# Convolution input turned and copied by halves of its output, with three reorderings around the down products

## The chip, the cores and the metric

The kernel runs on one core of a Trainium2 chip. The metric is the device time of one execution in microseconds (us). Engines are named as the profile names them: PE is TensorE (PEld its weight loads), DVE is VectorE, ACT is ScalarE, POOL is GpSimd, SP is SyncE, which issues the weight transfers here.

## The reference, cut to what matters

The program is a first transformer block followed by a block of two layers, over 256 tokens and 1024 channels, all in float32. The change touches one layer of the second block (it runs twice) and the last product of the first block:

```python
for i in range(2):                                     # second block
    h = h + 0.5 * swiglu(rms_norm(h), w_gate_up, w_down)      # "a", hidden width 2816
    u = rms_norm(h)
    q, k, v, ca, cg = split(u @ w_in)
    attn = sliding_window_attention(q, k, v)           # 8 heads of 64: 512 channels
    conv = silu(layer_norm(depthwise_conv31(ca * sigmoid(cg))))   # 512 channels, causal, 31 taps
    mixed = concat(rms_norm(attn), rms_norm(conv))
    h = h + mixed @ w_out
    h = h + 0.5 * swiglu(rms_norm(h), w_gate_up, w_down)      # "b"
    h = h + sigmoid(h @ w_gate) * rms_norm(p @ w_ple)
```

The first block ends with `h = h + square(relu(hn @ w_ff1)) @ w_ff2`, hidden width 4096.

## The kernel before, in words

**Weight products.** Every product with a weight matrix is a "chunk" (L2063 to L2087): 256 rows by 512 columns accumulated in one of two PSUM tiles `acc`, over k-tiles of 128. A float32 product is made of three matmuls (high by high, high by low, low by high: L2084 to L2086) for each of two row tiles, so 6 matmuls for a k-tile. Weights come in units of two k-tiles (12 matmuls). For each unit SP loads it into one of 8 `stage` slots (L550), ACT rounds it to `w_hi` (L671), DVE subtracts to `w_lo` (L1265), in one of 4 slots that PE must have used. All queues take the units in one fixed order. `Lout_a0` and `Lout_a1` (attention half of `w_out`), `Lout_c0` and `Lout_c1` (convolution half) and `Lple0`, `Lple1` have two units each, `Lb_up0` four.

**Turns.** Where a product needs its left side transposed, PE transposes 128 by 128 pieces into one of two PSUM banks `turn` (`turned`, L2089 to L2098), four pieces or 512 columns to a bank; ACT copies the bank out rounded (L741, L744), DVE writes the remainder (L1317, L1321). `turn_free` tells PE that a bank was read. The waits `ready(kt)` put such work between the k-tiles of a chunk.

**The convolution** (`conv`, L2510; `conv_round`, L2501). Two taps are applied by one matmul: `u_t` holds the turned input in quads of 32 partitions, 2k and 2k+1 being the same 32 channels shifted by one token. A round is 8 products on 64 rows by 32 columns of the array, side by side. The 8 channel groups fall in two halves of the output (`half`); each half takes 14 rounds with the diagonal weights `diag` and one with `y_late`, in which DVE has applied the last taps (`late_pair`, L1929 to L1938). The float32 round is recorded as 16 matmuls, the whole convolution as 480 in each layer. Before it, PE turns `u` in two banks (L2560), runs `Lple1`, waits until both are copied to `u_t`, and turns the attention output (`Lmixed`, L2564). Bank k holds channel tiles 2k and 2k+1, that is the quads 2k and 2k+1 of both halves, so that a half needs both banks. ACT makes half of the copies of each bank (L1178), DVE the other half (L1924), 4 copies of 32 by 512 each; DVE waits for ACT's and frees the bank (L1927 to L1929).

**After the convolution** ACT and DVE write `y` (L1193, L1951); PE runs `Lout_a0` with the mean over the channels between its k-tiles, then `Lout_a1`. ACT takes silu of `y` tile by tile and rounds it to `x_hi` (L1208, L1212), DVE writes `x_lo` (L1972), PE runs `Lout_c0` with the row means (L2598) between its units, then `Lout_c1`. ACT and DVE split both units of `Lout_c0` (L1204, L1968) before these loops, and DVE adds the result of `Lout_a0` to `h` (L1339) between its split and its loop.

**Boundaries** (`rms_boundary`, L703 on ACT, L1287 on DVE): at the end of a chunk pair DVE adds the second product to `h`, PE turns `h`, and the splits of the next chunk lie around this. `early` is 1 only where the last chunk has fewer than 4 units, which is `Lout_c1`.

**The last hidden turn.** A down product (`d0` in the first block, `La_dn0` and `Lb_dn0` in each layer) starts with hidden tiles that are already turned; the last hidden chunk is turned from inside it, when kt is UNIT_K = 2 (L2428 `last_ff`, L2475 `last_hid`), after waiting for DVE's L1765 or L1816.

## Time and profile before

| | us |
|---|---|
| median of 3 runs | 1474.58 (1474.26 to 1478.44) |
| profiled execution | 1474.51 |
| its span, first to last instruction | 1472.7 |
| PE busy | 1436.9 (98% of the span) |
| DVE busy, ACT busy | 878.1 (60%), 802.2 (54%) |
| DMA | 170 GB/s mean, queue q1 at 53.5% |
| granted TensorE clock, mean | 0.993 |

The second block's layers occupy about 450 to 960 and 960 to 1465 us of the span; the attention and convolution of the first lie at 648 to 735 us, those of the second at 1159 to 1246 us. Times below are us from the start of the span. A mean clock of 0.993 says that the engine ran at its upper level, 2.4 GHz, nearly all the time; 0.50 in a window is the lower level, 1.2 GHz. In a timeline row the first number is the start, the second the length of the group, the one in brackets the engine's idle time before it and what ended that.

### The profile page before, as it was taken

The numbers are of one execution on the slowest core, as the hardware profiler recorded it, in microseconds if no ns is written. First come the engines' busy times: TensorE is split into PE (matmuls) and PEld (weight loads), VectorE is DVE, ScalarE is ACT, GpSimd is POOL, SyncE is SP. The second block draws the span as 40 slices with busy tenths as digits, with TensorE's granted clock in tenths as the row PEclk, the third lists the DMA queues.
The fourth block names the chain that finished last, engine by engine and source line by source line (L and its number), as shares of the span: only waits on it lengthen the run. The fifth ranks groups of instructions, "written<-read, shape, count | busy, mean of one in ns | idle before, by whom it ended". The sixth has DMA issues, their size and how long they took to land.

```text
span 1472.7 us, 20845 instructions
## 1 busy us (share of the span) xinstructions
PE 1436.9 (98%) x7848; PEld 1185.6 (81%) x7848; DVE 878.1 (60%) x1154; ACT 802.2 (54%) x1227; POOL 15.8 (1%) x29
## 2 busy tenths in 40 slices
PE   8899999999999999999999999999999999999997
PEld 7788888888888888887788888888888877888885
DVE  4776766665545556556565555655564665655555
ACT  6678764654346444466564544564444765544444
POOL 2000000000000000000000000000000000000000
PEclk9999999999999999999999999999999999999998
DMA  9663354655666665552266656566555433665550
GB/s 244 198 210 115 115 176 153 214 175 168 194 189 206 185 182 179 161 169 96 88 209 185 185 176 205 177 187 185 185 185 158 144 115 100 199 185 183 189 188 29
DMA packets 133163, 249.89 MB, mean 170 GB/s; under 512 B 8752, under 2 KB 16496, under 8 KB 133088
## 3 DMA queue, kind: packets, MB, share of 16 engines
q1 hardware_dynamic: 131520, 245.09, 53.5%
q0 software_dynamic: 1360, 3.70, 1.3%
q8 instruction: 51, 0.84, 0.2%
q14 instruction: 24, 0.20, 0.0%
q10 hardware_dynamic: 208, 0.06, 0.0%
HBM read 247.77 MB, written 1.05 MB: 169 GB/s over the span
## 4 chain that ended last, share of the span: by engine, by line
PE 93%; DVE 2%; DMA 1%; ACT 1%; SPq 1%; issue 1%; DVEq 0%; ACTq 0%
PE acc L2084 28%; PE acc L2086 27%; PE acc L2085 27%; PE turn L2097 5%; PE pair L2506 2%; PE turn L2146 1%; DMA stage<-in_w_in 1%; PE pair L2125 1%; DVE w_lo L1265 1%; PE pair L2572 0%; SPq L550 0%; PE pair L2119 0%; DVE u_t L1924 0%; SPq L554 0%; ACT w_hi L671 0%
## 5 line engine op out<-in xcount | busy, mean ns | idle before, releaser
L1265 DVE TENSOR_TENSOR w_lo<-stage,w_hi 128x1024 fp32r<-128x1024 f32 (+2 forms) x480 | 563.9, 1184 | 396.5 <-ACT w_hi L671 391.5
L671 ACT ACTIVATE w_hi<-stage 128x1024 fp32r<-128x1024 f32 (+2 forms) x480 | 487.4, 1028 | 469.0 <-PE acc L2086 461.5
L2084 PE MATMUL acc<-w_hi,x_hi 128*128 128x512 f32 (+2 forms) x1296 | 514.0, 397 | 7.6 <-DVE w_lo L1265 5.0
L2086 PE MATMUL acc<-w_hi,x_lo 128*128 128x512 f32 (+2 forms) x1296 | 501.7, 387 | 0.0
L2085 PE MATMUL acc<-w_lo,x_hi 128*128 128x512 f32 (+2 forms) x1296 | 501.1, 387 | 0.0
L2084 PEld LDWEIGHTS acc<-w_hi,x_hi 128*128 128x128 f32 x1296 | 244.3, 188 | 58.2 <-issue 7.1
L2086 PEld LDWEIGHTS acc<-w_hi,x_lo 128*128 128x128 f32 x1296 | 244.0, 188 | 51.0
L2085 PEld LDWEIGHTS acc<-w_lo,x_hi 128*128 128x128 f32 x1296 | 244.6, 189 | 45.8 <-issue 0.2
L2084 PE MATMUL acc<-w_hi,g_hi 128*128 128x512 f32 x352 | 137.7, 391 | 0.0
L2086 PE MATMUL acc<-w_hi,g_lo 128*128 128x512 f32 x352 | 137.1, 389 | 0.0
L2085 PE MATMUL acc<-w_lo,g_hi 128*128 128x512 f32 x352 | 137.0, 389 | 0.0
L2086 PEld LDWEIGHTS acc<-w_hi,g_lo 128*128 128x128 f32 x352 | 66.1, 188 | 13.8
L2084 PEld LDWEIGHTS acc<-w_hi,g_hi 128*128 128x128 f32 x352 | 66.1, 188 | 13.6
L2085 PEld LDWEIGHTS acc<-w_lo,g_hi 128*128 128x128 f32 x352 | 66.1, 188 | 13.4
L744 ACT ACTIVATE x_hi<-turn,vec 128x256 fp32r<-128x256 f32 x72 | 28.6, 474 | 46.0 <-PE turn L2097 45.9
L2084 PE MATMUL acc<-w_hi,f_hi 128*128 128x512 f32 x128 | 50.0, 390 | 0.0
L2086 PE MATMUL acc<-w_hi,f_lo 128*128 128x512 f32 x128 | 49.8, 389 | 0.0
L2085 PE MATMUL acc<-w_lo,f_hi 128*128 128x512 f32 x128 | 49.8, 389 | 0.0
L1321 DVE SCALAR_TENSOR_TENSOR x_lo<-turn,vec,x_hi 128x256 fp32r<-128x256 f32 x72 | 30.0, 477 | 25.4 <-ACT x_hi L744 25.4
L1317 DVE TENSOR_TENSOR g_lo<-turn,g_hi 128x512 f32 (+1 forms) x44 | 30.0, 682 | 18.6 <-ACT g_hi L741 18.6
L1816 DVE SCALAR_TENSOR_TENSOR hid<-acc,stat,silu 128x256 f32<-128x256 f32 x88 | 38.2, 476 | 2.8 <-ACT silu L700 2.8
L741 ACT ACTIVATE g_hi<-turn 128x512 f32 (+1 forms) x44 | 26.3, 598 | 24.5 <-PE turn L2097 24.5
(323 smaller groups left out, 1146.9 us busy)
## 6 DMA issues: line engine op xcount, KB each, us to landing
stage<-in_ffn_w_gate_up SPq DMA_DIRECT2D x176, 512.0 KB, 3.7
stage<-in_ffn_w_down SPq DMA_DIRECT2D x88, 512.0 KB, 4.0
stage<-in_w_in SPq DMA_DIRECT2D x64, 512.0 KB, 4.3
stage<-in_w_ff SPq DMA_DIRECT2D x64, 512.0 KB, 4.3
stage<-in_w_out SPq DMA_DIRECT2D x16, 512.0 KB, 3.8
stage<-in_w_ple_gate SPq DMA_DIRECT2D x16, 512.0 KB, 4.5
stage<-in_w_lru_up SPq DMA_DIRECT2D x8, 512.0 KB, 4.1
stage<-in_w_o SPq DMA_DIRECT2D x8, 512.0 KB, 4.4
```

The costliest lines, as they stand in the source:

```text
L671: act.activation(w_hi[:, n.slot(SPLIT), 0:t, 0:w], stage[:, n.slot(STAGE), 0:t, 0:w], ACT.Copy).then_inc(hi_done, 1)
L741: act.activation(dst[:, bass.ds(at, 2), :], bank, ACT.Copy).then_inc(turn_hi, 1)
L744: ins = act.activation(dst[:, at + i, :], bank[:, i, :], ACT.Copy, scale=gain[:, at + i:at + i + 1])
L1265: dve.tensor_tensor(w_lo[:, n.slot(SPLIT), 0:t, 0:w], stage[:, n.slot(STAGE), 0:t, 0:w], w_hi[:, n.slot(SPLIT), 0:t, 0:w].bitcast(F32), AL ...
L1317: dve.tensor_tensor(lo[:, bass.ds(at, 2), :], bank, hi[:, bass.ds(at, 2), :].bitcast(F32), ALU.subtract).then_inc(turn_free[n.slot(2)], 1)
L1321: ins = dve.scalar_tensor_tensor(lo[:, at + i, :], bank[:, i, :], gain[:, at + i:at + i + 1], hi[:, at + i, :].bitcast(F32), ALU.mult, ALU ...
L1816: ins = dve.scalar_tensor_tensor(hid2[:, i % 2, t, :], acc[b][:, t, HALFW:COLS], stat[:, t:t + 1], silu[:, i % 2, t, :], ALU.mult, ALU.mult)
L2084: pe.matmul(dst, xh, wh, start=kt == 0, stop=False)
L2085: pe.matmul(dst, xh, wl, start=False, stop=False)
L2086: mm = pe.matmul(dst, xl, wh, start=False, stop=kt == last)
L2097: mm = pe.transpose(turn[n.slot(2)][0:cols_in, at:at + rows_in], src, ident[0:rows_in, 0:rows_in])
L2506: mm = pe.matmul(pair[c * QUAD:(c + 1) * QUAD, k, half * S:(half + 1) * S], weights(rows_in, n), src(rows_in, n), start=first, stop=last)
```

## The change

1. `u` is turned by halves: bank 0 gets channel tiles 0 and 2, bank 1 tiles 1 and 3, so that the bank holds all that one half of the convolution needs. A copy to `u_t` is 32 by 256 instead of 32 by 512, and ACT and DVE make 8 for a bank instead of 4 (`shifted_pairs`).
2. PE no longer waits for both banks ahead of the convolution. Each half waits for its own bank. The turns of `Lmixed`, which need both banks free, move from ahead of the convolution to between the 14 rounds of half 0 and its last round.
3. `Lout_c0`: ACT splits unit 1 after the third silu and second `x_hi` instead of ahead of the loop; DVE splits unit 1 after the second `x_lo`.
4. DVE's `rms_boundary` with `early` = 1 (`Lb_norm` only) adds the residual of `Lout_c1` before it splits unit 1 of `Lb_up0`, no longer after it.
5. The last hidden turn of `d0` and of each `dn0` moves from kt = 2 to kt = 4.

```diff
@@ -528,11 +528,14 @@
             for k in range(max(0, count - 2), count):
                 turn_read(eng, name, k, layer)
 
-        def shifted_pair(k, c, i):
-
-            quad = 2 * k + i
-            dst = u_t[quad * QUAD:(quad + 1) * QUAD, c::KC, TAPS2 - 1 - i:TAPS2 - 1 - i + S]
-            return dst, lambda bank: bank[c * QUAD:(c + 1) * QUAD, :].rearrange("p (n s) -> p n s", n=2)
+        def shifted_pairs(half, blocks, bank):
+
+            for c in blocks:
+                for k in range(2):
+                    for i in range(2):
+                        quad, at = 2 * k + i, TAPS2 - 1 - i
+                        yield (u_t[quad * QUAD:(quad + 1) * QUAD, half * KC + c, at:at + S],
+                               bank[c * QUAD:(c + 1) * QUAD, k * S:(k + 1) * S])
 
         block = ctx.enter_context(nc.Block())
 
@@ -1172,10 +1175,8 @@
                 for k in range(2):
                     n = TURNS.at("Lu", k, layer)
                     wait(act, turn_done, n + 1)
-                    for c in range(KC // 2):
-                        for i in range(2):
-                            copy_to, copy_from = shifted_pair(k, c, i)
-                            ins = act.activation(copy_to, copy_from(turn[n.slot(2)]), ACT.Copy)
+                    for copy_to, copy_from in shifted_pairs(k, range(KC // 2), turn[n.slot(2)]):
+                        ins = act.activation(copy_to, copy_from, ACT.Copy)
                     ins.then_inc(s_shifted, 1)
                 for k in range(2):
                     turned_hi(x_hi, "Lmixed", k, vec2[:, layer, V2["attn"]:V2["attn"] + 4], layer)
@@ -1201,7 +1202,7 @@
                 act.wait_ge(s_sqattn, layer + 1)
                 rows = stat[:, STATS["attn"]:STATS["attn"] + TT]
                 act.activation(rows, rows, ACT.Sqrt, bias=eps).then_inc(s_rattn, 1)
-                split("Lout_c0", layer)
+                split("Lout_c0", layer, units=[0])
                 wait(act, s_yn, Count(1, [(layer, 1)]))
                 for n in range(KC + 1):
                     if n < KC:
@@ -1211,6 +1212,8 @@
                         wait(act, s_silu, Count(n, [(layer, KC)]))
                         act.activation(x_hi[:, 4 + n - 1, :], y[:, n - 1, :], ACT.Copy,
                                        scale=vec2[:, layer, V2["conv"] + n - 1:V2["conv"] + n]).then_inc(s_convhi, 1)
+                    if n == 2:
+                        split("Lout_c0", layer, units=[1])
                 act.activation(ysq[:, :, :], y[:, :, :], ACT.Square).then_inc(s_ysq, 1)
                 embedding_squares(1)
                 wait(act, score_done, SCORES.at("Lsum", 3, layer))
@@ -1299,9 +1302,9 @@
                 for k in (0, 1):
                     turned_lo(hi, lo, norm, k, gain, layer)
                 split(parts[1], layer, units=range(min(n_last, a + 3), n_last))
-                split(first, layer, units=range(early, 2))
+                split(first, layer, units=range(early, 2 - early))
                 add_residual(parts[1], 1, scale, layer)
-                split(first, layer, units=range(2, 3))
+                split(first, layer, units=range(2 - early, 3))
                 for k in (2, 3):
                     turned_lo(hi, lo, norm, k, gain, layer)
                 split(first, layer, units=range(3, U))
@@ -1918,10 +1921,8 @@
                 for k in range(2):
                     n = TURNS.at("Lu", k, layer)
                     wait(dve, turn_done, n + 1)
-                    for c in range(KC // 2, KC):
-                        for i in range(2):
-                            copy_to, copy_from = shifted_pair(k, c, i)
-                            ins = dve.tensor_copy(copy_to, copy_from(turn[n.slot(2)]))
+                    for copy_to, copy_from in shifted_pairs(k, range(KC // 2, KC), turn[n.slot(2)]):
+                        ins = dve.tensor_copy(copy_to, copy_from)
                     link(ins)
                     wait(dve, s_shifted, Count(k + 1, [(layer, 2)]))
                     dve.sem_inc(turn_free[n.slot(2)], 1)
@@ -1965,12 +1966,14 @@
                 wait(dve, s_rattn, Count(1, [(layer, 1)]))
                 at = STATS["attn"]
                 link(dve.reciprocal(stat[:, at:at + TT], stat[:, at:at + TT]))
-                split("Lout_c0", layer)
+                split("Lout_c0", layer, units=[0])
                 add_residual("Lout_a0", 0, stat[:, at:at + TT], layer)
                 for n in range(KC):
                     wait(dve, s_convhi, Count(n + 1, [(layer, KC)]))
                     dve.scalar_tensor_tensor(x_lo[:, 4 + n, :], y[:, n, :], vec2[:, layer, V2["conv"] + n:V2["conv"] + n + 1],
                                              x_hi[:, 4 + n, :].bitcast(F32), ALU.mult, ALU.subtract).then_inc(s_convlo, 1)
+                    if n == 1:
+                        split("Lout_c0", layer, units=[1])
                 add_residual("Lout_a1", 1, stat[:, at:at + TT], layer)
 
                 def conv_factors():
@@ -2425,7 +2428,7 @@
                 if kt == 0:
                     for m in range(2):
                         turn_read(pe, "ff", 2 * (NF - 2) + m)
-                elif kt == UNIT_K:
+                elif kt == 2 * UNIT_K:
                     ff_turns(NF - 1)
                 elif kt == KF1 - COLS // P:
                     for m in range(2):
@@ -2476,7 +2479,7 @@
 
                     if kt == 0:
                         turn_read(pe, f"L{f}_hid", UPS - 2, layer)
-                    elif kt == UNIT_K:
+                    elif kt == 2 * UNIT_K:
                         hid_turns(UPS - 1)
                     elif kt == KF2 - HALFW // P:
                         turn_read(pe, f"L{f}_hid", UPS - 1, layer)
@@ -2510,9 +2513,13 @@
                 def conv():
 
                     for half in range(2):
+                        turn_read(pe, "Lu", half, layer)
                         for j in range(PAIRS_PE):
                             conv_round(half, lambda rows_in, n: diag[rows_in, n, j, :],
                                        lambda rows_in, n: u_t[rows_in, n, 2 * j:2 * j + S], j == 0, False)
+                        if half == 0:
+                            turns_read(pe, "Lu", 2, layer)
+                            turn_rows("Lmixed", mixo2, 2, layer)
                         wait(pe, s_late_taps, Count(half + 1, [(layer, 2)]))
                         mm = conv_round(half, lambda rows_in, n: quad_ident[rows_in, :],
                                         lambda rows_in, n: y_late[rows_in, n, :], False, True)
@@ -2557,11 +2564,10 @@
                 turn_read(pe, "Lp", 0, layer)
                 chunk("Lple0", pl_hi, pl_lo, layer)
                 evacuated(pe, "Lca", layer)
-                turn_rows("Lu", u, 2, layer)
+                for half in range(2):
+                    turned("Lu", half, [u[:, t, f * P:(f + 1) * P] for f in (half, 2 + half) for t in range(TT)], layer)
                 chunk("Lple1", pl_hi, pl_lo, layer)
-                turns_read(pe, "Lu", 2, layer)
                 wait(pe, s_mixo, Count(2, [(layer, 1)]))
-                turn_rows("Lmixed", mixo2, 2, layer)
                 wait(pe, s_diag, Count(1, [(layer, 1)]))
                 free(SCORES, score_free, "Lsum", 0, layer)
                 conv()
```

## Rows read from the trace of the kernel before

**Rows 1.** The page: busy time of each engine, its share, and instructions.
```profile
PE 1436.9 (98%) x7848; PEld 1185.6 (81%) x7848; DVE 878.1 (60%) x1154; ACT 802.2 (54%) x1227; POOL 15.8 (1%) x29
```

**Rows 2.** Waits of PE, 230 to 1460 us: in total, times, longest.
```profile
PE turn L2097 <- DVEq L1927: 5.9, 2, 3.0
PE turn L2097 <- issue: 4.7, 7, 1.1
```

**Rows 3.** Timeline around the convolution, first layer.
```profile
687.55 2.80 DVE L1924 COPY u_t<-turn 32x512 f32<-32x512 f32 x4 [2.91 <-PE turn L2097]
688.07 4.79 ACT L1178 ACTIVATE u_t<-turn 32x512 f32<-32x512 f32 x8
...
693.58 1.94 PE L2097 MATMUL turn<-ct,mixo 128*128 128x128 f32 x8 [2.96 <-DVEq L1927]
...
695.45 7.00 PE L2506 MATMUL pair<-u_t,diag 64*32 64x256 f32 x224
...
710.86 0.19 PEld L2084 LDWEIGHTS acc<-w_hi,x_hi 128*128 128x128 f32 x1 [0.41 <-issue]
```

**Rows 4.** Windows: length, PE busy and instructions, then clock, DMA share, GB/s last.
```profile
693.50:695.50 2.00, 1.92 (x16) 1.62 (x20) 1.90 (x6) 0.80 (x2) 0.00 (x0) 0.52 0.03 8
695.50:711.00 15.50, 14.79 (x482) 10.17 (x482) 8.70 (x18) 7.04 (x15) 0.00 (x0) 0.95 0.34 105
...
1205.60:1221.80 16.20, 15.89 (x483) 10.27 (x483) 9.93 (x22) 7.74 (x18) 0.00 (x0) 0.90 0.32 100
...
354.00:356.00 2.00, 0.86 (x8) 1.00 0.95 331
```

**Rows 5.** Tile `y`: durations (min/median/max ns) of reads of 128x256 from PSUM.
```profile
L1193 ACT ACTIVATE y<-pair,vec x4: 467/472/475, 711.0 to 1221.8; 128x256 f32<-128x256 f32 x4
L1951 DVE TENSOR_SCALAR y<-pair,vec x4: 473/480/485, 711.0 to 1221.8; 128x256 f32<-128x256 f32 x4
```

**Rows 6.** Timeline of ACT and DVE beside the convolution, first layer.
```profile
693.57 1.14 DVE L1935 TENSOR_SCALAR pt<-u_t,taps 128x256 f32<-128x256 f32 x4 [0.18 <-DVE u_t L1924]
...
694.70 1.69 ACT L744 ACTIVATE x_hi<-turn,vec 128x256 fp32r<-128x256 f32 x4 [1.84 <-PE turn L2097]
...
696.34 2.35 DVE L1265 TENSOR_TENSOR w_lo<-stage,w_hi 128x1024 fp32r<-128x1024 f32 x2
...
702.35 0.21 ACT L1127 ACTIVATION_READ_ACCUMULATOR hid<-e_ple 128x1 f32 x1
```

**Rows 7.** Timeline around `Lout_c0`, first layer.
```profile
722.40 2.36 DVE L1265 TENSOR_TENSOR w_lo<-stage,w_hi 128x1024 fp32r<-128x1024 f32 x2
...
722.64 1.09 ACT L1208 ACTIVATE y<-y,vec 128x256 f32<-128x256 f32 x2
...
726.22 1.04 ACT L1214 ACTIVATE sm<-y 128x1024 f32<-128x1024 f32 x1
...
726.86 0.47 PE L2084 MATMUL acc<-w_hi,x_hi 128*128 128x512 f32 x1 [1.29 <-DVE x_lo L1972]
...
728.50 1.28 ACT L1217 ACT_TABLE_LOAD   x1
...
732.79 2.36 DVE L1265 TENSOR_TENSOR w_lo<-stage,w_hi 128x1024 fp32r<-128x1024 f32 x2 [3.56 <-ACT w_hi L671]
```

**Rows 8.** Timeline at the end of `Lout_c1`, first layer.
```profile
741.40 1.23 DVE L1265 TENSOR_TENSOR w_lo<-stage,w_hi 128x1024 fp32r<-128x1024 f32 x1 [1.24 <-ACT w_hi L671]
...
742.54 1.40 DVE L1339 SCALAR_TENSOR_TENSOR h<-acc,stat,h 128x512 f32<-128x512 f32 x2
...
744.11 1.06 PE L2097 MATMUL turn<-ct,h 128*128 128x128 f32 x8 [0.61 <-issue]
```

**Rows 9.** Timeline at the start of `d0`.
```profile
351.37 0.39 PE L2084 MATMUL acc<-w_hi,f_hi 128*128 128x512 f32 x1
...
355.39 1.06 PE L2097 MATMUL turn<-ct,hid 128*128 128x128 f32 x8 [1.14 <-issue]
...
358.12 1.22 DVE L1265 TENSOR_TENSOR w_lo<-stage,w_hi 128x1024 fp32r<-128x1024 f32 x1
```

## The prediction

> **What bounds the kernel now.** The page first: PE is busy 98% of the span, DVE and ACT 60% and 54% [rows 1]. PE sets the time, so the change can only gain by what PE stands still or runs slowly, and all of it is worth reading one by one. The waits of PE between 230 and 1460 us come next [rows 2]. Two kinds matter: 5.9 us in two waits behind L1927, where DVE frees the banks of `u`, and 4.7 us in seven waits ahead of a turn that the profile calls "issue". The timelines tell what those seven are: one of 1.14 at `d0` [rows 9], two of 0.61 at the `Lb_norm` boundary [rows 8], and the other four are the last hidden turns of the `dn0` chunks: (4.7 - 1.14 - 1.22) / 4 = 0.58 each. In all of them PE waits for a DVE result that comes just too late. A last one stands ahead of `Lout_c0`, 1.29 us, for `x_lo` [rows 7]. Then the windows for the clock [rows 4]: it falls to its lower level only around the convolution, after PE stood still for 2.96 us [rows 3].
>
> The profiled execution (1474.51, span 1472.7) is within 0.1 us of the median of the runs, so the sum is made against 1474.5. What a measurement of this kernel can tell from no change is about 0.3%, 4.4 us.
>
> **1. The wait ahead of the convolution.** Before: `Lple1` ends at 693.58 - 2.96 = 690.62, the turns of `Lmixed` begin at 693.58, the convolution runs from 695.45 to 710.86, 15.4 us [rows 3]. After, PE needs only bank 0. ACT starts to copy at 688.07 and DVE at 687.55, as now. They make 8 copies of 32x256 each. No row has that copy. Bounds: not under half of today's 32x512, 4.79/8 = 0.60 on ACT and 2.80/4 = 0.70 on DVE [rows 3], which is 0.30 and 0.35; not above the whole, 0.60 and 0.70. The nearest rows are the reads of 128x256 from PSUM, also in pairs, 472 ns on ACT and 480 on DVE alone [rows 5], and two of them back to back take 0.84 and 0.88, so 0.42 and 0.44 a piece. I take these: ACT ends at 688.07 + 8 x 0.42 = 691.4, DVE at 691.1, and PE goes 0.2 later as now (693.39 to 693.58), at 691.6. The stall is 1.0 instead of 2.96: 2.0 gained.
> The two banks together now cost 16 x 0.44 = 7.0 on DVE and not 5.8, and 6.7 on ACT and not 4.8. The copy of half a row at 0.42 instead of 0.30 shows a fixed cost for each instruction. The Trainium skill (VectorE: DVE Perf Modes, the section on the TRN2 errata) has the same rule against small pieces and gives 120 and 172 fixed cycles for a read from PSUM. From its figures the pieces would be 0.39 on DVE and 0.36 on ACT, an estimate that would let PE start 0.5 us earlier and make the result 1461.3; it also puts today's 32x512 at 0.66 and 0.57, under the 0.70 and 0.60 of the trace, so I stay with the rows.
>
> **2. The clock.** In the first layer the granted clock is 0.52 over 2.0 us and 0.95 over 15.5: 1.9 + 1.55 = 3.5 us at 1.2 GHz. In the second it is 0.90 over 16.2 us: 3.2 us [rows 4]. Work done at half speed costs half of that, 1.7 us a layer. It begins right behind the 2.96 us of idle time. Idle times of 1.14 (in the window from 354, at 1.00 [rows 4]) and 1.29 us bring no fall, and the new stall is 1.0, so I count it as gone: 1.65 a layer.
>
> **3. The turns of `Lmixed` in the convolution.** Their 1.06 us at full clock stay PE work. What is new is that PE leaves the 64x32 tiles and comes back. The only row of such a switch is the first full weight load behind the convolution, 0.41 idle [rows 3]; I put two switches at 0.4 together, bounds 0 and 0.8.
> Nothing else may wait. DVE finishes bank 1 at 691.2 + 3.5 = 694.9 with its handovers; the late taps of a half take 693.57 to 696.34 = 2.8 [rows 6], so those of half 0 are there at 697.9. PE comes to them at 691.6 + 14 rounds + turns. The convolution at full clock is 15.4 less 0.8 (half of 1.55) = 14.6 with 0.9 of gaps in the first layer, 13.7 without: 30 rounds of 0.46. So half 0 ends at 698.0, the turns at 699.2: DVE is early by 1.3, and that is what moving the turns there covers. The half-1 taps follow after the split of `Lout_a0`, at 697.9 + 2.35 + 2.8 = 703.1; PE wants them at 705.9.
> On ACT everything behind `turned_hi` for `Lmixed` is queued behind the later turns: 694.70 to 702.56, 7.9 us [rows 6]. It now begins at 698.8 and ends at 706.7; PE ends the convolution at about 707. ACT then writes `y`. It is a tie, with 0.4 us more before PE asks for `y` (one k-tile of `Lout_a0`, 6 matmuls, comes first). I count nothing.
> Together, a layer: 2.0 + 1.65 - 0.4 - 0.2 for ties and handovers = 3.0. Check by positions: PE at 690.6 + 1.0 + 13.7 + 0.9 + 1.1 + 0.4 = 707.7 against 710.9, 3.2. I take 3.0; two layers, **6.0**. Bounds, for the two layers: 1.2 (copies as dear as today's, a stall of 2.7, half of the clock's gain, 0.4 for the switches) and 9 (copies at half of today's, a stall of 0.1, free switches).
>
> **4. `Lout_c0`.** DVE now does one unit (1.18, half of 2.36) from 722.40, the residual of 1.4, and the first `x_lo` of 0.48: it ends at 725.6 and not 726.7, and PE starts 1.1 earlier. The second split goes between; PE needs it two k-tiles later, at 728.5. ACT: the first silu no longer waits for a second split (it starts at 722.3, when `y` is ready, not 722.64), but the loop to 726.22 grows by 1.0 for the split, so the squares L1214 run from 726.9 to 728.0, just ahead of the row means at 728.5; the unit's `w_hi` is done at 725.8 and `w_lo` at 727.3. Next late is ACT's table load: now at 728.50, then at 729.3 to 730.6, which puts the square root and the first split of `Lout_c1` at 730.8. Its `w_lo`, now at 732.79, starts at 731.9. So 0.9 of the 1.1 is kept [rows 7]. Two layers, **1.8**, bounds 0.5 and 2.6.
>
> **5. The boundary.** A unit is four half k-tiles of 3 matmuls: in `d0` two k-tiles take 354.25 - 351.37 = 2.88 with the tail of the last matmul, 2.75 from start to start [rows 9]. PE ends the first unit of `Lb_up0` at 744.11 - 0.61 = 743.5 [rows 8], so `Lout_c1` ended at 740.65. DVE today waits for `w_hi` (741.3), splits to 742.54, adds to 743.94, and PE turns at 744.11. After: the residual runs at 740.85 to 742.25, the split at 742.3 to 743.5, and PE needs both. It waits for the split, to 743.65. Gain 0.45; two layers, **0.9**, bounds 0 and 1.2.
>
> **6. The hidden turns.** At kt = 4 the DVE result is over 2 us old, so the whole idle time goes: 1.14 + 4 x 0.58 = **3.5**. Cover for it is the unit of weight work now put ahead of the turn. Behind it are ACT's and DVE's copies of the turn and then the fifth unit's split, queued behind the later turn: in `d0` its `w_lo` starts at 358.12 now [rows 9], then about 359.7 and is done at 360.9. PE asks for it at kt = 8, 351.4 + 8 k-tiles of 1.375 + 1.06 = 363.4 [rows 9]. Free by 2.5 us. The turned tile itself is used near the end of the chunk.
>
> No weight load moves in the order of SP. The loads follow DVE's splits, and at 53% of the DMA there is room for a kernel under 1% shorter.
>
> **Sum.** 6.0 + 1.8 + 0.9 + 3.5 = 12.2. 1474.5 - 12.2 = **1462.3**.
>
> **The rivals.**
> - *The clock still falls.* The short stall is followed by work on small tiles. For: in the second layer it fell about 1 us after PE had restarted. Against: idle times of 1.1 and 1.3 us without a fall. Price 1.65 x 2: 1465.6. Chance 0.12. The Trainium skill (TensorE: Matmul & The Clock Gate, the section on what is happening) says that the point of change shifts with where the work lands; this trace has it at two different points.
> - *Copies do not get cheaper by halves.* 0.60 and 0.70: bank 0 is done at 693.2, the stall is 2.7 and the clock falls again. (1.7 + 1.65) x 2 lost: 1469.0. Chance 0.04.
> - *Something is late next.* ACT's tie in part 3, its squares or table load in part 4, or a fifth unit in part 6; each would take 1 to 3.5 back, say 1464.8. Chance 0.12.
> - *Slower: the clock stays low through the convolution.* With turns in the middle and 64x32 tiles at both sides PE might be granted 1.2 GHz for all of `conv`: at half speed its 13.7 us of work take 27.4, so 1462.3 + 2 x 13.7 = 1489.7. It ends above the time of before once the loss is over 12.2 / 2 = 6.1 us a layer, that is once the low clock lasts over 12.2 us in each. Against: the convolution now runs at 1.00 for its last 12 us, on the same tiles. Chance 0.02.
>
> **How the numbers follow.** My forecast has 0.70. The range goes down by what cheaper copies and free switches could add, and part of the spread of part 4, to 1459.5, and up over the clock and the late rivals to 1467.0; copies at today's price and the slow case stay outside. Faster by over 0.3% (under 1470.1) holds all but the slow rival and some of the unseen: 0.94, same 0.03, slower 0.03.
>
> **What would show it.** Right: waits behind DVE at the start of `conv` of about 1.0 and not 2.96; windows there at 1.00; no idle time ahead of the `hid` turns; idle ahead of `Lout_c0` under 0.3 and about 0.3 ahead of `Lout_c1`; 32x256 copies of 0.42 to 0.44. Wrong: a clock of 0.5 in the convolution, a wait of L2506 for the late taps, ACT's `y` starting over 0.4 us after the last round, or a stall at kt = 8 of a `dn0`.

## The result, and the profile after

The changed kernel takes 1458.76 us (median of 4 runs, 1457.99 to 1459.28) against 1474.76 before (median of 4): ratio 0.989, 95% interval 0.9872 to 0.9907, so 16.0 us faster. Beside other kernels later it took 1458.33 against 1473.53, ratio 0.9896 (0.9875 to 0.9917). The forecast was 1462.3 with a range from 1459.5 to 1467.0: the direction and the places were right, the gain of 12.2 was a quarter too small, and the result lies 0.7 us under the range. The changed kernel's profiled execution took 1459.28, its span is 1457.5.

The page of the changed kernel, busy time ([rows 1] before), then its waits of PE between 225 and 1450 us, in total, times, longest ([rows 2]):

```profile
PE 1432.0 (98%) x7848; PEld 1185.7 (81%) x7848; DVE 880.2 (60%) x1170; ACT 803.6 (55%) x1243; POOL 15.8 (1%) x29
```

```profile
PE pair L2509 <- DVEq L1928: 1.4, 2, 0.7
PE pair L2509 <- issue: 0.6, 1, 0.6
PE acc L2087 <- DVE x_lo L1973: 0.3, 2, 0.2
PE turn L2100 <- DVE w_lo L1268: 0.3, 2, 0.2
```

Five of the seven waits ahead of turns are gone and the two at the boundary have shrunk from 0.61 to 0.16; the wait for the banks has shrunk from 5.9 to 1.4, that for `x_lo` from 2.6 to 0.3. One line names no other engine: 0.6 "issue" inside the convolution, idle time of PE for which the profile shows no cause; below it is called a gap. The kernel before has such gaps too:

```profile
PE pair L2506 <- issue: 0.9, 2, 0.6
```

The timeline around the convolution, first layer, changed kernel ([rows 3] and [rows 6]); PE, DVE and ACT:

```profile
686.35 3.49 DVE L1925 COPY u_t<-turn 32x256 f32<-32x256 f32 x8 [2.90 <-PE turn L2100]
686.87 6.15 ACT L1179 ACTIVATE u_t<-turn 32x256 f32<-32x256 f32 x16
690.05 3.49 DVE L1925 COPY u_t<-turn 32x256 f32<-32x256 f32 x8 [0.21 <-ACT u_t L1179]
...
690.11 6.28 PE L2509 MATMUL pair<-u_t,diag 64*32 64x256 f32 x224 [0.70 <-DVEq L1928]
693.73 1.14 DVE L1936 TENSOR_SCALAR pt<-u_t,taps 128x256 f32<-128x256 f32 x4 [0.18 <-DVE u_t L1925]
...
696.32 1.09 PE L2100 MATMUL turn<-ct,mixo 128*128 128x128 f32 x8
...
697.02 1.57 ACT L747 ACTIVATE x_hi<-turn,vec 128x256 fp32r<-128x256 f32 x4 [4.00 <-PE turn L2100]
697.35 0.18 PEld L2509 LDWEIGHTS pair<-pt,vec 64*32 64x32 f32 x16 [0.17 <-issue]
...
703.35 1.73 PE L2509 MATMUL pair<-u_t,diag 64*32 64x256 f32 x54 [0.63 <-issue]
...
705.66 0.50 PE L2087 MATMUL acc<-w_hi,x_hi 128*128 128x512 f32 x1
705.80 0.84 ACT L1194 ACTIVATE y<-pair,vec 128x256 f32<-128x256 f32 x2 [1.06 <-PE pair L2509]
```

The copies of one bank take 3.49 on DVE (0.44 a piece) and half of 6.15 on ACT (0.38 a piece). PE begins the convolution 0.70 after `Lple1`, turns `Lmixed` in the middle with nothing idle on either side, and ACT is free 1.06 before it may write `y` (in the second layer 0).

Windows of the changed kernel over the convolution and its turns, both layers ([rows 4]): length, then busy time and instructions of PE, PEld, DVE, ACT, POOL, then granted clock, DMA share, GB/s:

```profile
690.10:705.60 15.50, 14.86 (x488) 11.21 (x488) 13.96 (x31) 10.56 (x24) 0.00 (x0) 1.00 0.23 73
1194.00:1208.20 14.20, 14.20 (x488) 10.95 (x488) 13.82 (x31) 10.12 (x23) 0.00 (x0) 1.00 0.24 77
```

The clock is at its upper level in both windows. (In both kernels it also stands at 1.2 GHz at about 50 us, 0.55 and 0.53 granted between 49 and 56 us, and at the very end; no part of the change is there.) The same 488 instructions take 1.3 us longer in the first layer; an experiment below bears on why.

The other places in the changed kernel: `Lout_c0` and its splits ([rows 7]), the boundary ([rows 8]) and the turn in `d0` ([rows 9]):

```profile
717.12 1.10 ACT L1209 ACTIVATE y<-y,vec 128x256 f32<-128x256 f32 x2 [0.65 <-DVE y L1964]
...
719.41 1.05 ACT L674 ACTIVATE w_hi<-stage 128x1024 fp32r<-128x1024 f32 x1
...
720.52 0.47 PE L2087 MATMUL acc<-w_hi,x_hi 128*128 128x512 f32 x1 [0.16 <-DVE x_lo L1973]
720.69 1.22 DVE L1268 TENSOR_TENSOR w_lo<-stage,w_hi 128x1024 fp32r<-128x1024 f32 x1
...
725.23 0.26 ACT L1220 ACTIVATE stat<-pair,ct 128x2 f32<-128x2 f32 x1
...
726.48 2.36 DVE L1268 TENSOR_TENSOR w_lo<-stage,w_hi 128x1024 fp32r<-128x1024 f32 x2 [2.46 <-ACT w_hi L674]
...
737.32 1.09 PE L2100 MATMUL turn<-ct,h 128*128 128x128 f32 x8 [0.16 <-DVE w_lo L1268]
...
357.74 1.03 PE L2100 MATMUL turn<-ct,hid 128*128 128x128 f32 x8
...
359.35 2.01 ACT L674 ACTIVATE w_hi<-stage 128x1024 fp32r<-128x1024 f32 x2
```

**Where the time went.** Both kernels run the same 5616 weight matmuls in the same order, so the difference in the start times of the same matmul can be followed through the program. It is flat, to 0.05 us, between the edited places, and steps at them. (The first 90 us differ from one execution to the next; there the changed kernel's execution lost 0.93.)

| place | forecast | step, layer 1 | step, layer 2 | sum |
|---|---|---|---|---|
| convolution, last matmul of `Lple1` to first of `Lout_a0` | 3.0 a layer | 4.00 | 4.68 | 8.7 |
| `Lout_c0` | 0.9 a layer | 1.12 | 1.10 | 2.2 |
| boundary `Lb_norm` | 0.45 a layer | 0.42 | 0.43 | 0.85 |
| hidden turn of `d0` | 1.14 | 1.34 | | 1.3 |
| hidden turns of the `dn0` | 0.58 each | 0.73, 0.74 | 0.74, 0.73 | 2.9 |

The sum is 16.0. What is left open is why each is larger than its row of idle time.

### The profile page after: what moved, and what is told of

It reads as the page before. It is cut to its first block, busy times and chain, and to the rows that moved or that the text cites. A ratio compares the mean times of both kernels' runs of the same rounds, so it can differ in the third digit from the quotient of the medians.

```text
span 1457.5 us, 20877 instructions
## 1 busy us (share of the span) xinstructions
PE 1432.0 (98%) x7848; PEld 1185.7 (81%) x7848; DVE 880.2 (60%) x1170; ACT 803.6 (55%) x1243; POOL 15.8 (1%) x29
## 4 chain that ended last, share of the span: by engine, by line
PE 93%; DVE 2%; ACT 2%; DMA 1%; SPq 1%; issue 1%; DVEq 0%; ACTq 0%
PE acc L2087 28%; PE acc L2089 27%; PE acc L2088 27%; PE turn L2100 5%; PE pair L2509 2%; PE turn L2149 1%; DMA stage<-in_w_in 1%; PE pair L2128 1%; DVE w_lo L1268 1%; ACT w_hi L674 1%; PE pair L2578 0%; SPq L553 0%; ACT u_t L1179 0%; PE pair L2122 0%; SPq L557 0%
```

## The experiments

The theory to begin with: (a) the standstill itself makes the clock fall, and both together are most of the gain; (b) a wait that vanishes is worth more than its idle time; (c) nothing is taken back by leaving the small tiles. Its rivals stand in the expectations. "Stage" below is the time from the last matmul of `Lple1` to the first of `Lout_a0`, start to start; "work" is the part of it from the first turn of `Lmixed` or the first round; "start to start" is the time between the starts of two matmuls.

| kernel | wait, layers 1 and 2 | work, layer 1 | work, layer 2 |
|---|---|---|---|
| before | 2.96, 2.96 | 17.29 | 16.71 |
| changed | 0.70, 0.70 | 15.55 | 14.30 |
| both banks awaited | 4.48, 4.47 | 15.67 | 15.99 |
| order of before, new copies | 4.48, 4.48 | 18.32 | 17.50 |
| before, wait filled | 1.64 after the filling | 14.45 | 15.42 |
| one more switch | 0.70, 0.70 | 15.23 | 14.62 |
| loads held back | 0.70, 0.70 | 14.31 | 14.30 |
| input turned earlier, first and second run | none | 14.59, 14.38 | 14.35, 14.30 |

### Both banks awaited

```diff
                 free(SCORES, score_free, "Lsum", 0, layer)
+                turns_read(pe, "Lu", 2, layer)
                 conv()
```

> The changed kernel, but PE waits for both banks of the turned input ahead of the convolution; the turns of Lmixed stay in its middle. Both theories: the convolution starts when DVE has copied the second bank, 693.54 + 0.27 = 693.8 instead of 690.1, so 3.7 us more a layer. Theory (the clock falls because PE stands still for some us): it falls again at the start of the convolution, for some 3.3 us at 1.2 GHz in each layer, 1.65 more a layer, together 10.7 over the changed kernel: 1469.5. Rival (the fall came from the turns that stood between the wait and the convolution, and these are gone from there): the clock stays at 1.00 and the time is 1458.8 + 7.4 = 1466.2.

Measured: 1468.81 (10 runs), ratio to before 0.9966 (0.9952 to 0.998). Windows over the convolution of this kernel:

```profile
691.60:707.20 15.60, 15.59 (x488) 10.92 (x488) 10.55 (x23) 7.32 (x15) 0.00 (x0) 0.91 0.26 77
1199.40:1215.40 16.00, 15.95 (x488) 12.12 (x488) 10.58 (x23) 7.36 (x15) 0.00 (x0) 0.89 0.25 73
```

PE waits 4.5 us and the clock falls again, without any turn between wait and convolution: in both layers 3.41 us at 1.2 GHz (added up from windows of 0.5 us). The rival falls. The stage is 5.5 longer in the second layer, near what was expected (3.8 of waiting and 1.7 of clock), and 3.9 in the first, where the gap of the changed kernel is missing and part of the low clock lay in the wait.

### Order of before, new copies

```diff
-                        if half == 0:
-                            turns_read(pe, "Lu", 2, layer)
-                            turn_rows("Lmixed", mixo2, 2, layer)
...
+                turns_read(pe, "Lu", 2, layer)
+                turn_rows("Lmixed", mixo2, 2, layer)
                 conv()
```

> The changed kernel with PE's order of before around the convolution (both banks, then the turns of Lmixed, then all rounds), so only the smaller copies are left of that part. Theory (a 32x256 copy carries most of the cost of a 32x512 one): both banks take 16 x 0.436 on DVE, 7.0 and not 5.8, PE stands still for 4.3 us a layer instead of 2.96, and the stage is 1.4 us a layer slower than in the kernel before; the rest of the change keeps its gain of about 7.4: near 1470.2. Rival (halves cost no more in sum, since the engines are bound by the elements): the stage is as before, 1467.4.

Measured: 1471.94 (10 runs), ratio 0.9983 (0.9968 to 0.9997). Its waits, and a window of the second layer:

```profile
PE turn L2100 <- DVEq L1928: 9.0, 2, 4.5
PE pair L2509 <- issue: 1.7, 2, 1.4
```

```profile
1204.10:1221.60 17.50, 17.29 (x488) 11.14 (x488) 10.51 (x23) 7.83 (x16) 0.00 (x0) 0.84 0.30 93
```

The wait is 1.52 longer than before, so halving the copies alone is a loss, and the longer wait costs clock too: in the second layer 6.8 us at 1.2 GHz. The stage is 2.6 and 2.3 us slower a layer than in the kernel before, not 1.4: the theory is right, its size was off by the gaps (1.4 and 0.3 idle in the first layer here) and, in the second layer, by the clock. Only together with the reordering do the smaller copies pay.

### The wait filled in the kernel before

```diff
                 chunk("Lple1", pl_hi, pl_lo, layer)
+                free(SCORES, score_free, "Lsum", 0, layer)
+                keep_warm(12)
                 turns_read(pe, "Lu", 2, layer)
                 wait(pe, s_mixo, Count(2, [(layer, 1)]))
                 turn_rows("Lmixed", mixo2, 2, layer)
                 wait(pe, s_diag, Count(1, [(layer, 1)]))
-                free(SCORES, score_free, "Lsum", 0, layer)
```

> The kernel before, with 12 transposes of the identity into an unused part of PSUM in the wait of PE ahead of the turns of Lmixed, so that PE is busy in it; nothing else is changed. Theory (the standstill makes the clock fall): PE starts the turns at the same place, the clock stays at 1.00 in the convolution, and the 3.5 and 3.2 us at 1.2 GHz cost nothing: 1.7 a layer less, 1474.7 - 3.4 = 1471.3. Rival (the fall comes with the small tiles or by chance): the clock falls as before and the time is 1474.7, or more if the transposes last longer than the wait.

Measured: 1470.76 (10 runs), ratio 0.9982 (0.9966 to 0.9997). The windows of this kernel over the wait of the first layer and over both convolutions, then PE's timeline in the wait:

```profile
691.00:694.10 3.10, 1.51 (x13) 1.23 (x11) 2.77 (x4) 2.37 (x5) 0.00 (x0) 1.00 0.00 0
694.10:708.60 14.50, 14.45 (x489) 11.44 (x489) 10.60 (x23) 7.72 (x16) 0.00 (x0) 1.00 0.37 113
1202.20:1217.60 15.40, 14.88 (x488) 10.45 (x488) 10.61 (x23) 7.72 (x16) 0.00 (x0) 1.00 0.34 105
```

```profile
691.03 1.47 PE L2154 MATMUL pair<-ct 128*128 128x128 f32 x12
694.15 1.06 PE L2097 MATMUL turn<-ct,mixo 128*128 128x128 f32 x8 [1.64 <-issue]
695.14 6.27 PE L2506 MATMUL pair<-u_t,diag 64*32 64x256 f32 x224
701.21 0.63 PE L2506 MATMUL pair<-pt,vec 64*32 64x256 f32 x16
701.64 6.38 PE L2506 MATMUL pair<-u_t,diag 64*32 64x256 f32 x221
```

The turns start at the same distance from `Lple1` as before (3.35 us), the wait is as long, but half of it is filled with useless work, and the clock stays at 1.00. The stages are shorter by 2.8 and 1.3 us, together 4.1. This isolates the clock: 3.41 us at half speed cost 1.7 us in each layer of the kernel before, 3.4 in all, and it was the standstill that brought them; the rest, and the uneven shares, are gaps in the issue (one of 0.43 in the second layer here). An idle time of 1.64 us did not.

One trace stands for each kernel here, and the fall need not come in every execution. The medians differ by 2.5 us (1473.21 against 1470.76), less than the 4.1 of the two traces. The 43 executions of the kernel before that were timed beside these kernels spread from 1468.4 to 1478.9 us: 11 with a mean granted clock of 0.995 or more took 1468.4 to 1473.5, 13 with 0.992 or less 1472.8 to 1478.9. Ten executions of the changed kernel lie between 1456.9 and 1459.3, all at 0.995 or 0.996. The low stretch at the start of the program varies too (3.4 to 6.8 us in a piece), so the mean clock alone does not tell where the clock fell.

This trace also gives the price of the place of the turns. With the turns ahead, from their start to the first round of half 1 it takes 701.64 - 694.15 = 7.49 us, in both layers. With the turns between rounds 14 and 15 it takes 697.80 - 690.11 = 7.69 in the changed kernel, in both layers and in both of its traces:

```profile
697.80 4.92 PE L2509 MATMUL pair<-u_t,diag 64*32 64x256 f32 x164
```

So leaving the small tiles and coming back costs 0.2 us a layer, though the profile shows nothing idle there. The rest of the work takes 6.61 where there is no gap. At the upper clock and without gaps the order of before would thus need 14.1 us (7.49 + 6.61) and the changed one needs 14.30. What is above that and above the 1.7 of the clock is gaps: 1.5 and 0.9 us in the two layers of the kernel before, 1.25 and 0 in the changed one.

### Hidden turns back

```diff
-                elif kt == 2 * UNIT_K:
+                elif kt == UNIT_K:
                     ff_turns(NF - 1)
...
-                    elif kt == 2 * UNIT_K:
+                    elif kt == UNIT_K:
                         hid_turns(UPS - 1)
```

> The changed kernel with the last hidden turn of d0 and of each dn0 back at kt = 2. The forecast's sum takes the idle time of the waits as the price: 1.14 + 4 x 0.58 = 3.5, so 1462.3. Theory (a stall costs more than the idle time shown, since a matmul's recorded 0.39 overlaps the next by 0.16 and the pipeline restarts): 1.41 in d0 and 0.74 in each dn0, 4.4 in all, 1463.2. In the trace the first matmul after the turn would stand 1.4 and 0.75 later against the matmul before it than in the changed kernel.

Measured: 1461.39 (4 runs), ratio 0.9915 (0.9887 to 0.9943). Its timeline in `d0`:

```profile
354.76 1.06 PE L2100 MATMUL turn<-ct,hid 128*128 128x128 f32 x8 [1.14 <-issue]
```

Idle times of 1.14 and 0.58 are back, and the start times step by 1.34 and by 0.74, 0.75, 0.75, 0.77: 4.35 in all. The theory holds on the size. Weight matmuls follow each other at 0.23 us but are recorded as 0.39 long, so the idle time in the profile begins 0.16 late, and each wait that vanishes is worth 0.16 to 0.2 more than it shows.

### Splits of `Lout_c0` back, boundary back

```diff
-                split("Lout_c0", layer, units=[0])
+                split("Lout_c0", layer)
...
-                    if n == 2:
-                        split("Lout_c0", layer, units=[1])
```

(the same on DVE), and in the other kernel

```diff
-                split(first, layer, units=range(early, 2 - early))
+                split(first, layer, units=range(early, 2))
                 add_residual(parts[1], 1, scale, layer)
-                split(first, layer, units=range(2 - early, 3))
+                split(first, layer, units=range(2, 3))
```

> The changed kernel with both units of Lout_c0 split ahead of the loops again, on ACT and on DVE. Theory (a wait costs its idle time and the 0.16 by which a recorded matmul overlaps the next, and ACT's table load takes nothing back): the stage from Lout_a1 to the start of Lout_c1 is 1.12 longer in each layer, 2.2 in all. Rival, as the forecast had it (the table load makes the first split of Lout_c1 late and takes 0.2 back): 0.9 a layer, 1.8 in all.

> The changed kernel with DVE's split of unit 1 of Lb_up0 ahead of the residual again. Forecast and theory agree: 0.42 to 0.45 longer a layer at the turn in Lb_up0, 0.85 in all, with an idle time of 0.6 ahead of that turn. Rival (the gain there came from the earlier stages): nothing is lost.

Measured, one time each: 1462.61 and 1458.33, with the first 90 us of the span 1.4 longer in the one and 1.5 shorter in the other than in the changed kernel's first trace. The steps against the changed kernel are clean: 1.13 and 1.12 at `Lout_c0` in the first, 0.44 and 0.44 at the turn in `Lb_up0` in the second. The waits of the first show what came back:

```profile
PE acc L2083 <- DVE x_lo L1971: 2.6, 2, 1.3
```

Nothing is taken back by the table load: in the changed kernel it ends at 725.22, just as the row means do, the square root follows at 725.23, and the first `w_lo` of `Lout_c1` is done at 727.7, 0.2 before PE starts that chunk at 727.9.

### One more switch of tiles

```diff
                         for j in range(PAIRS_PE):
+                            if half == 0 and j == 10:
+                                turns_read(pe, "Lu", 2, layer)
+                                turned("Lmixed", 0, pieces(mixo2, 0), layer)
                             conv_round(...)
                         if half == 0:
-                            turns_read(pe, "Lu", 2, layer)
-                            turn_rows("Lmixed", mixo2, 2, layer)
+                            turned("Lmixed", 1, pieces(mixo2, 1), layer)
```

> The changed kernel with the two turns of Lmixed at two places of half 0, after 10 rounds and after 14, so that PE leaves the small tiles once more and comes back; the work is the same. Forecast (two switches cost 0.4): 0.4 longer a layer. Theory (a switch costs nothing that can be read, since the convolution of the changed kernel shows no gap at its own): under 0.1 a layer, apart from gaps in the issue of the convolution, which vary from 0 to 1.3 us from run to run.

Measured: 1460.92, one time. Work in the second layer 14.62 against 14.30. PE's timeline there:

```profile
1195.40 4.55 PE L2509 MATMUL pair<-u_t,diag 64*32 64x256 f32 x160 [0.70 <-DVEq L1928]
1199.88 0.66 PE L2100 MATMUL turn<-ct,mixo 128*128 128x128 f32 x4
1200.47 1.96 PE L2509 MATMUL pair<-u_t,diag 64*32 64x256 f32 x64
1202.36 0.66 PE L2100 MATMUL turn<-ct,mixo 128*128 128x128 f32 x4
1202.95 0.66 PE L2509 MATMUL pair<-pt,vec 64*32 64x256 f32 x16
```

In the first layer the work is 15.23, as in three kernels with one switch less (hidden turns, splits and boundary back: 15.23, 15.22, 15.23), but with a gap that is 0.3 shorter. Leaving the tiles and coming back once more costs 0.3 in the layer without gaps, half of it in the turns themselves (0.59 + 0.59 start to start, against 1.02 for both together). The theory's "under 0.1" is wrong as a general price; 0.4 was nearly right for a second switch. At the place of the change the price is the 0.2 us read from the kernel with the filled wait.

### Loads held back

```diff
+                wait(sp, s_conv, Count(1, [(layer, 1)]))
                 swiglu_loads("b", layer)
```

> The changed kernel, but SP holds the loads of Lb_up0 back until the convolution is over. Theory on the gaps in the issue of the convolution (0.9 to 1.3 in the first layer of most traces, with no wait on another engine): the fetch of PE's instructions is late behind the burst of weight loads at 698 to 703 us. Then the convolution with its turns takes 14.3 in the first layer too, 0.9 to 1.2 less, and nothing else changes. Rival (the gaps have nothing to do with the loads): they stay, 15.2 to 15.6 in the first layer.

Measured: 1457.6, one time. In the changed kernel the gap follows a stretch in which the weight queue fills the DMA engines and one fetch of instructions (q8) stands between its packets. The DMA queues there, 700 to 702 us: packets, MB, share:

```profile
q1 hardware_dynamic: 382, 0.75, 99.0%
q8 instruction: 1, 0.02, 2.7%
```

With the loads held back, PE's timeline in the first layer is

```profile
697.33 6.25 PE L2510 MATMUL pair<-u_t,diag 64*32 64x256 f32 x224
703.37 0.64 PE L2510 MATMUL pair<-pt,vec 64*32 64x256 f32 x16
```

The 224 matmuls of half 1 come in one piece, the work is 14.31 in the first layer as in the second, 1.24 less than in the changed kernel, and no other stage moves. It ran once; the six other traces that begin and order the convolution like the changed kernel have 0.9 to 1.5 us of gaps in the first layer. So the gaps there come from the weight loads beside the convolution. The loads alone are not enough: the second layer of the changed kernel has them too (0.24 of the DMA engines' time) and no gap, nor has either layer with both banks awaited.

The packets of q8 in the traces tell more. All eleven gaps of over 0.25 us inside a convolution, in nine traces, end 1.4 to 1.6 us after a fetch of instructions has landed. In the changed kernel's first layer the fetch ahead of the gap, the third of the convolution, of 16 KB, starts 11.0 us after the convolution's start; with the loads held back the third starts 9.0 us after it. That PE's own instructions are late behind the weights is thus the likely way, but the trace does not say whose fetch q8 is.

### The convolution alone, and the changed kernel again

The first is the kernel before with parts 1 and 2 of the change only.

> The kernel before with the first two parts of the change alone: input turned and copied by halves, turns of Lmixed in the convolution. The forecast's term is 6.0: 1468.7. Theory (the idle time falls by 2.26 a layer, the clock gives 1.7, and nothing is taken back): 3.96 a layer plus what the gaps in the issue do, 8 to 8.7 in all, 1466.4. If the parts did not add up, the stages behind it would differ from those of the kernel before by over 0.1.

> The changed kernel once more, beside the others of this set: 1458.8, 1.1% under the kernel before. Both theories: between the matmuls the same stage lengths as in its first trace to 0.1 us, except for the start of the program (the first 90 us) and for gaps in the issue of the convolution.

Measured in one set: 1465.24 (6 runs), ratio 0.9944 (0.9923 to 0.9965), and 1458.33 (6 runs), ratio 0.9896 (0.9875 to 0.9917). The steps of the first against the kernel before are 4.29 and 4.67, and nowhere else over 0.05; what it lacks against the changed kernel is 1.34 + 4 x 0.74, 2 x 1.12 and 2 x 0.42. The parts add up; the time is under the 1466.4 of the theory and 3.5 under the forecast's 1468.7. The changed kernel's second trace differs from its first by 0.26 in the gap of the first layer and nowhere else behind the start.

### A faster version: the input turned earlier

What is left of the wait is 0.70 a layer, and it is set by when the copies start. `u` is ready before `Lple0`. So bank 0 is turned there (`turn_input` holds the turn of one half), and ACT splits `Lout_a0` after its copies:

```diff
-                chunk("Lple0", pl_hi, pl_lo, layer)
                 evacuated(pe, "Lca", layer)
-                for half in range(2):
-                    turned("Lu", half, [u[:, t, f * P:(f + 1) * P] for f in (half, 2 + half) for t in range(TT)], layer)
+                turn_input(0)
+                chunk("Lple0", pl_hi, pl_lo, layer)
+                turn_input(1)
...
-                split("Lout_a0", layer)
                 act.wait_ge(s_zero, 3)
                 for k in range(2):
...
+                split("Lout_a0", layer)
```

> The changed kernel with bank 0 of the input turned ahead of Lple0 and bank 1 behind it, and ACT's split of Lout_a0 behind its copies. Theory (what is left of the wait is 0.70 of idle time and 0.2 that the idle time does not show, and only the copies' start sets it): DVE and ACT start on bank 0 three us earlier, the wait is gone and a layer is 0.9 shorter, 1.8 in all, 1457.0. Rival (another engine is late next: late taps, Lple1, or ACT's queue behind the later splits): a new wait of 0.5 or more inside Lple1 or the convolution, and no gain.

> The changed kernel with bank 0 of the input turned ahead of Lple0, once more, beside the changed kernel of the same set: 0.71 less in the second layer's stage, and about the same in the first's apart from the gaps, so 1.4 to 2 us under the changed kernel of this set.

Measured: 1457.57 (4 runs), ratio 0.9891 (0.9874 to 0.9907); again, beside the changed kernel's 1458.33: 1455.7 (5 runs), ratio 0.9883 (0.9859 to 0.9906). Timeline of the second run ahead of the convolution, first layer:

```profile
680.85 0.61 PE L2100 MATMUL turn<-ct,sm 128*128 128x128 f32 x4
...
681.55 6.20 ACT L1178 ACTIVATE u_t<-turn 32x256 f32<-32x256 f32 x16 [1.54 <-PE turn L2100]
681.69 3.49 DVE L1925 COPY u_t<-turn 32x256 f32<-32x256 f32 x8 [0.21 <-DVE mixo L1407]
684.04 0.60 PE L2100 MATMUL turn<-ct,sm 128*128 128x128 f32 x4
...
687.34 0.88 PE L2509 MATMUL pair<-u_t,diag 64*32 64x256 f32 x24
```

The wait is gone and no other took its place. The stage is 0.71 and 0.77 shorter in the second layer in the two runs, not the 0.9 expected: a switch from `Lple1` straight to the small tiles takes 0.32 start to start. In the first it is 1.72 and 1.94 shorter, where the gaps have shrunk too (work 14.59 and 14.38), and the start of `Lple0` and `Lple1` gives 0.05 a layer. It is the fastest kernel of this study; its margin over the changed one, 2.6 us by the medians of one set and 1.5 to 1.6 by the steps of the second layer taken twice, is near what a measurement can tell, but the steps in both traces have the same sign and nearly the same size. Together with held-back loads it was not tried.

## Why the prediction was right or wrong

The mechanism and all five places were right. What failed is the sum at the convolution: 3.0 a layer forecast, 4.00 and 4.68 measured. It left the gaps at what they were and took off 0.4 for switches and 0.2 for ties, and it priced vanishing waits elsewhere by idle time. The missing 3.8 us are: gaps 1.1, switches and ties 0.8, hidden turns 0.8, the wait 0.5, `Lout_c0` 0.4, and 0.2 for the clock and for rounding 3.05 to 3.0.

- **Gaps.** Not in the sum except as unchanged (0.9 in the first layer). With 30 rounds of 0.43 and not 0.46, they were 1.5 and 0.9 us in the kernel before, and 1.25 and 0 in the changed one: 1.1 of the missing part, the largest piece. Nothing in the forecast aimed at it, and no run shows why the new order has no gap in the second layer; it is luck as far as the forecast goes. Without it the time would have been 1459.9, inside the range.
- **Switches and ties.** Mis-sized: 0.4 for two switches and 0.2 for ties were taken off, and the runs show 0.2 for the switches and nothing for ties. That is 0.8 of the missing part. The 0.41 idle of the weight load that I took the 0.4 from is there for every first full load behind the tiles, and PE's matmuls do not wait that long: the turns start at 696.32, before the recorded end of the last round at 696.39. The tie on ACT was one: in the first layer, with a gap in PE's rounds, ACT has 1.06 to spare, in the second none at all, and as forecast PE asks for `y` late enough for it to cost nothing.
- **Hidden turns.** All idle time gone and nothing late behind them, as forecast. The term was mis-sized: 3.5 by idle times, 4.3 by start times, since a vanished wait is worth 0.16 to 0.2 more than it shows. That is 0.8 of the missing part, and the same 0.16 is not in the others, where a little wait is left.
- **Wait ahead of the convolution.** Right in kind, too small. Predicted 1.0 left and 2.0 gained; 0.70 left and 2.26 gained, 0.5 in two layers. The price of an ACT copy was too high: 0.42 taken from the reads with a bias, 0.38 measured, so that ACT, which I had last, is done with DVE at 689.9; DVE's 0.44 was exact. The Trainium skill (VectorE: DVE Perf Modes, the section on the TRN2 errata) would have, as an estimate from its fixed cycles, 0.36 for ACT and 0.39 for DVE: nearer on ACT, too low on DVE. Its wait of 0.5 misses the measured 0.70 by 0.2, mine of 1.0 by 0.3, on the other side.
- **`Lout_c0`.** Forecast 0.9, measured 1.12: 0.4 in two layers. The 0.2 taken back by the table load did not come: the forecast had it end last, and on the chip it ended at 725.22, within 0.05 us of the row means.
- **Clock.** Right: 1.65 predicted, 1.7 by the traces, gone in the changed kernel and brought back by waits of 4.5. That the fall belongs to the standstill was an inference then and is shown now; that it fell only around the convolution was misread, since it also falls at about 50 us and at the end. The Trainium skill (TensorE: Matmul & The Clock Gate, the section on what is happening) ties the low level to idle stretches, and the traces agree (idle times of 2.96 and 4.48 us ended in 1.2 GHz, 0.70 to 1.64 did not); the first rival, a fall in spite of the short wait, did not come in any of the ten traces with 0.70 or none.
- **Boundary.** Right: 0.45 against 0.42; the split is what it now waits for, 0.16 idle.
- **The range** failed at its lower end because the errors nearly all had one sign: places carried a deduction for something that might go wrong (1.2 for switches and ties, 0.4 for the table load), and these were summed as if they were expected; and the gaps, which could shrink, had no part in it.

## What to carry to other kernels

Price a wait by the start times of the matmuls around it, and add what it does to the clock behind it; here 2.96 us of idle time cost nearly 5 in the traces. If two halves of a stage need two halves of an input, arrange the input by the halves, even if its copies get smaller and dearer in sum (16 x 0.44 instead of 8 x 0.70), as long as the second half hides behind the first. Do not take off sums for small hazards at each place; put them into the range.

## What the runs showed of the hardware

- In the traces, standstills of TensorE of 2.96 and 4.48 us each came with 3.41 us at 1.2 GHz (6.8 in one case), which began between 1.3 us before the engine went on and 1.0 us after; ones of 0.70 to 1.64 us came with none. Twelve useless transposes in the wait kept the clock up, which is worth 3.4 of the 4.1 us by which the two stages of the kernel before became shorter.
- A straight run of small matmuls (about 35 a us) was held up in most traces by gaps of 0.3 to 1.4 us when weight loads filled the DMA at the same time, each ending 1.4 to 1.6 us after a fetch of instructions had landed. Holding these loads back removed all of it in the one run that tried.
- Leaving 64x32 tiles for eight 128x128 transposes and coming back cost 0.2 us more than doing the transposes first; a second such trip cost 0.3. No idle time shows either.
- A copy of 32x256 from PSUM took 0.44 on DVE and 0.38 on ACT, against 0.70 and 0.60 for 32x512: by these pairs about 0.17 of each is for the instruction (an estimate).
